# Moving the low half of every sixth expert weight quarter from VectorE to GpSimd

## The reference, cut to what matters

```python
def hier_moe(h, w_rg, b_rg, w_re, b_re, w1, w3, w2):
    """Top-1 group, then top-2 experts inside the chosen group; weight = p_group * p_expert."""
    ...
    comb = jnp.sum(jax.nn.one_hot(eid, N_EXPERTS, dtype=jnp.float32) * wts[..., None], axis=1)
    act = jax.nn.silu(jnp.einsum("nd,edf->nef", xt, w1)) * jnp.einsum("nd,edf->nef", xt, w3)
    act = act * comb[:, :, None].astype(act.dtype)
    y = jnp.einsum("nef,efd->nd", act, w2)
    return y.reshape(bsz, s, d)
```

## Time and profile before

| What | Value |
|---|---|
| median of three runs | 809.09 us (809.0 to 810.13) |
| the profiled execution, its own time | 808.32 us |
| its span | 806.3 us |
| mean granted TensorE clock | 0.993 of full speed |
| TensorE matmul busy | 787.6 us (98%) |
| VectorE busy | 468.5 us (58%) |
| ScalarE busy | 435.6 us (54%) |
| GpSimd busy | 449.2 us (56%), of which 9.59 us after 600 us |
| expert stage | from about 614 us to 799 us of the span |

### The profile page before, as it was taken

One profiled execution on the slowest core, in us unless ns is written; L12 is line 12 of the kernel. 1 busy time (PEld: TensorE's weight loads), 2 busy tenths in 40 slices (PEclk: granted clock), 3 DMA queues, 4 the chain that ended last, 5 costly groups with the idle time before them and its releaser, 6 DMA issues.

```text
span 806.3 us, 15714 instructions
## 1 busy us (share of the span) xinstructions
PE 787.6 (98%) x6063; PEld 705.5 (88%) x6063; DVE 468.5 (58%) x947; ACT 435.6 (54%) x680; POOL 449.2 (56%) x351
## 2 busy tenths in 40 slices
PE   9999999999999999999999999999998999999996
PEld 8999889999999998889999999999986878788784
DVE  5753454672412215486498944437638796795874
ACT  5434654745545456785449533234426675674753
POOL 4997486999999997877974524245832000000002
PEclk9999999999999999999999999999998999999998
DMA  8765145455654554445663312132406896696721
GB/s 296 270 209 209 59 151 183 160 207 208 208 208 163 202 206 165 159 150 179 201 202 119 106 54 90 70 106 106 144 1 270 356 355 270 239 400 230 297 87 52
DMA packets 22522, 148.14 MB, mean 184 GB/s; under 512 B 2624, under 2 KB 3136, under 8 KB 5568
## 3 DMA queue, kind: packets, MB, share of 16 engines
q1 hardware_dynamic: 21024, 144.11, 49.1%
q10 hardware_dynamic: 1440, 3.21, 1.3%
HBM read 144.82 MB, written 1.05 MB: 181 GB/s over the span
## 4 chain that ended last, share of the span: by engine, by line
PE 92%; DVE 4%; DMA 1%; ACT 1%; issue 1%; SPq 0%; DVEq 0%; ACTq 0%
PE bank L1268 77%; PE bank L1839 3%; DMA raw<-weights_dram 1%; DVE w_lo L3038 1%; PE bank L1421 1%; PE bank L1435 1%; PE bank L1371 1%; PE bank L1868 0%; PE bank L2083 0%; PE bank L1927 0%; PE bank L2123 0%; PE bank L1444 0%; PE bank L1445 0%; PE bank L1533 0%; PE bank L1809 0%
## 5 line engine op out<-in xcount | busy, mean ns | idle before, releaser
L659 POOL TENSOR_TENSOR w_lo<-raw,w_hi 128x512 fp32r<-128x512 f32 x340 | 439.5, 1328 | 151.8 <-ACT w_hi L711 141.7
L1268 PE MATMUL bank<-h_hi,w_hi 128*128 128x256 f32 x800 | 227.8, 285 | 0.1
L1268 PE MATMUL bank<-h_hi,w_lo 128*128 128x256 f32 x800 | 222.8, 279 | 0.0
L1268 PE MATMUL bank<-h_lo,w_hi 128*128 128x256 f32 x788 | 219.0, 278 | 0.0
L711 ACT ACTIVATE w_hi<-raw 128x1024 fp32r<-128x1024 f32 x170 | 173.6, 1059 | 65.2 <-PE bank L1268 34.9
L1268 PEld LDWEIGHTS bank<-h_hi,w_hi 128*128 128x128 f32 x800 | 150.6, 188 | 4.5 <-issue 1.7
L1268 PEld LDWEIGHTS bank<-h_hi,w_lo 128*128 128x128 f32 x800 | 150.5, 188 | 0.0
L1268 PEld LDWEIGHTS bank<-h_lo,w_hi 128*128 128x128 f32 x788 | 148.4, 188 | 0.3
L1268 PE MATMUL bank<-w_hi,g 128*128 128x512 f32 x360 | 115.8, 392 | 3.2 <-issue 1.6
L690 POOL TENSOR_TENSOR tok<-x_sb,work 128x512 f32<-128x512 f32 x2 | 2.5, 1288 | 185.6 <-DVE x_sb L3142 185.6
L1268 PEld LDWEIGHTS bank<-w_hi,g 128*128 128x128 f32 x360 | 67.6, 188 | 17.7 <-issue 2.0
(11 more groups left out here) (421 smaller groups left out, 1314.8 us busy)
## 6 DMA issues: line engine op xcount, KB each, us to landing
raw<-weights_dram SPq DMA_DIRECT2D x108, 1024.0 KB, 4.8
work<-weights_dram SPq DMA_DIRECT2D x24, 1024.0 KB, 6.9
raw<-weights_dram SPq DMA_DIRECT2D x4, 512.0 KB, 5.9
x_sb<-x_dram SPq DMA_DIRECT2D x2, 512.0 KB, 4.4
work<-final_norm_dram ACTq DMA_DIRECT2D x2, 512.0 KB, 3.9
work<-work ACTq DMA_DIRECT2D x8, 128.0 KB, 6.5
out_dram<-tok SPq DMA_DIRECT2D x3, 256.0 KB, 2.3
work<-constants_dram SPq DMA_DIRECT2D x1, 640.0 KB, 6.9
```

Of the source, the lines that this page charges most:

```text
L659: return nc.gpsimd.tensor_tensor(w_lo[:, part], raw[:, part], w_hi[:, part].bitcast(F32), ALU.subtract)
L1268: ins = mm(dst, a, b, start=start and n == 0, stop=stop and n == 2, skip_group_check=True)
```

## The change

The low half of every quarter with q = 5, 16 of the 96, is made by GpSimd in one instruction of 1024 columns. VectorE makes the other 80. GpSimd takes them in stream order behind `tok_lo`, each when the high half of that quarter is done. The semaphore `tok_lo_done` is renamed `pool_lo_done` and counts on from 2. TensorE waits for the semaphore of the engine that makes the quarter; SP waits for both before it loads over a raw half. What each quarter computes, the rings, the order on ScalarE and the steps of TensorE stay as they are.

```diff
+POOL_QUARTERS = (5,)
+
+def by_pool(j):
+    return STREAM[j][1] in POOL_QUARTERS
+
+def lows(j, pool):
+    return sum(by_pool(i) == pool for i in range(j + 1))
...
                 if h >= SLOT_RING:
-                    sp.wait_ge(sem("slot_lo_done"), 2 * (h - SLOT_RING) + 2)
+                    last = 2 * (h - SLOT_RING) + 1
+                    sp.wait_ge(sem("slot_lo_done"), lows(last, False))
+                    if lows(last, True):
+                        sp.wait_ge(sem("pool_lo_done"), NT + lows(last, True))
...
-                ins.then_inc(sem("tok_lo_done"), 1)
+                ins.then_inc(sem("pool_lo_done"), 1)
+            for j in range(len(STREAM)):
+                if by_pool(j):
+                    (hi_, lo_), of = slot_ring(j), slot_quarter(j)
+                    pool.wait_ge(sem("slot_hi_done"), j + 1)
+                    nc.gpsimd.tensor_tensor(lo_, of, hi_.bitcast(F32), ALU.subtract).then_inc(sem("pool_lo_done"), 1)
...
+            def await_low(j):
+                if by_pool(j):
+                    pe.wait_ge(sem("pool_lo_done"), NT + lows(j, True))
+                else:
+                    pe.wait_ge(sem("slot_lo_done"), lows(j, False))
...
                     else:
-                        pe.wait_ge(sem("slot_lo_done"), j + 1)
+                        await_low(j)
...
-                pe.wait_ge(sem("slot_lo_done"), j + 1)
+                await_low(j)
...
-            pe.wait_ge(sem("slot_lo_done"), len(STREAM))
+            for k in range(2):
+                await_low(streamed(LAST_UNIT, 4 + k))
...
-                    if p == SPLIT_AT[j]:
+                    if p == SPLIT_AT[j] and not by_pool(j):
                         slot_low(j)
```

More of the change, by code:

```diff
@@ L687, in _ @@
                 pool.wait_ge(sem("expert_constants"), 32)
-                pool.wait_ge(sem("tok_lo_done"), NT)
+                pool.wait_ge(sem("pool_lo_done"), NT)
                 pool.wait_ge(sem("x_summed"), c + 5)
@@ L2130, in _ @@
                 if p == 2:
-                    pe.wait_ge(sem("tok_lo_done"), NT)
+                    pe.wait_ge(sem("pool_lo_done"), NT)
                     gather(tok_lo, False, True)
```

## The result

The changed kernel takes 815.16 us (median of four runs, 813.74 to 817.13), the kernel before 809.05 in the same comparison: a ratio of 1.0079, with a 95% interval from 1.0065 to 1.0093. It is slower by 6.1 us. 815.6 us had been forecast, by the case of turns at SBUF and at least one fall of TensorE's clock. One execution further down, of the changed kernel with later splits, took 3419.99 us; nothing on record explains it, and its ratio leaves it out.

A forecast was written before the change was run, and what follows sets the result against it. TensorE, busy 98% of the span, was taken as the bound. Longer stalls (3.2 us), lost time between bunches (0.1) and clock falls (3.2) summed to 6.5 us on 809.09: 815.6 us, range 811.2 to 819.0.

The forecast's parts named there:

- the case of turns at SBUF and at least one fall of TensorE's clock: Likeliest case: GpSimd and VectorE alternate at SBUF, stalls grow, clock falls after two of three; 815.6 us, chance 0.50.
- The bound and the three places: TensorE busy 98%; stalls before down steps of units 2, 8 and 14, behind large bunches of low halves, are what matters.
- The turns: VectorE's two-input SBUF low halves and GpSimd's exclude each other; one GpSimd turn costs VectorE 2.2 us.
- The delay of a bunch: VectorE's low halves before units 2, 8 and 14: 2.2 added, 1.14 removed, +1.07 us each, 3.2 us for three.
- The length of GpSimd's instruction: GpSimd's low half of 1024 columns: between 2.27 and 2.57 us, taken as 2.4 us.
- The rival in which VectorE keeps the port: GpSimd waits until the low halves before units 2, 8 and 14 are done; 1.7 us faster, 807.4 us, chance 0.07.
- The clock: TensorE's clock falls to 1.2 GHz behind two of three stalls, 1.6 us each: 3.2 us, ends 0 and 4.8.
- Between the bunches: VectorE catching up in the units after each large stall: 0.1 us lost in all.
- The walk: VectorE's time between activation low halves against TensorE's allowance: 8.93 against 8.94 us for unit 3, 8.54 against 8.43 for unit 4.
- The sum: Whole kernel: 3.2 + 0.1 + 3.2 = 6.5 us over the median of 809.09, giving 815.6 us.
- the case's own range: Likeliest case: 813.8 us with one clock fall to 817.8 us with three and a longer GpSimd instruction.
- What could be gained: Stalls before units 2, 8 and 14: about 4.6 us removable in all; without added turns, 0.57 us gained at each.

The follow-up runs named there:

- later splits: Changed kernel with every split at the earliest four steps ahead of its first use, not up to six: 806.17 us, ratio 0.9962.
- the kernel with three handovers: Changed kernel with GpSimd making only quarters 15, 45 and 75, VectorE the other 93: 815.43 us, ratio 1.0064.
- the one with thirteen: Changed kernel with GpSimd making the q = 5 quarters except 15, 45 and 75, which stay on VectorE: 810.16 us, ratio 1.0006.
- where TensorE was kept busy: Changed kernel plus 16 zero-weight matmuls before TensorE's wait for the activation's low half of units 2, 8 and 14: 812.84 us, ratio 1.0055.
- the two pieces: Changed kernel with each GpSimd low half made in two instructions of 512 columns: 814.99 us, ratio 1.0076.
- the low half left out: Changed kernel with no engine making q = 5 low halves; GpSimd fills one column and signals, TensorE takes the high half twice: 807.76 us, ratio 0.9978.
- the fill: Changed kernel with GpSimd filling 1728 unused SBUF columns instead of making q = 5 low halves; TensorE takes the high half twice: 807.13 us, ratio 0.9968.

## Why the prediction was right

**The bound and the three places.** Right. Only the waits in front of the down steps of units 2, 8 and 14 mattered, as the kernel with three handovers shows from one side and the one with thirteen from the other.

**The turns.** Right, in kind and in size at the places that counted. The delay of a bunch was worked out as 2.2 - 1.14 = 1.07 us. It is 1.07 in the first bunch of the changed kernel, and 1.06, 1.08 and 1.07 where TensorE was kept busy. The length of GpSimd's instruction, bounded by 2.27 and 2.57 and taken at 2.4 us, is 2.40; the estimate of 2.36 drawn from a page lay near it too. The stalls of 2.5 to 2.7 us are 2.44, 2.73 and 2.67. The rival in which VectorE keeps the port is out for the bunches: in all three GpSimd went in when the low half before it ended (quarters 14, 44 and 74), and VectorE stood without a high half at that moment. It does happen elsewhere, in the 4.58 us at 673.46, where it helped and cost nothing.

**The clock.** Right that it falls, and the price of 1.6 us is that of the profile (2.69 - 1.08 and 2.66 - 1.07). That it would be after two of three stalls was a guess. In the three kernels with bare stalls of this length (the changed one, the three handovers, the two pieces) it fell at 5 of 9, once for 6.6 us and more, and twice the fall began before TensorE had resumed. At the twelve stalls of 0.79 to 1.64 us in the kernels before, with thirteen quarters, with the low half left out and with the fill it did not fall. The Trainium skill (TensorE: Matmul & The Clock Gate, section "HAM oscillation — how this bites in real kernels") warns only of longer idle gaps than these, and by it the clock would have held; here the runs speak against it.

**Between the bunches.** Under-sized. The step gave 0.1 us in all; the profile has 0.29 + 0.12, and 0.86 where the clock was held. The walk itself came true for unit 3: from one activation low half to the next it is 661.88 - 652.94 = 8.94 us, 8.93 forecast. But a wait that is missed by a hair has a price of its own, which the walk put at nothing:

```profile
661.94 0.39 PE L1289 MATMUL bank<-w_hi,slot_lo 128*128 128x512 f32 x1
662.35 0.50 PE L1289 MATMUL bank<-w_hi,g 128*128 128x512 f32 x1
```

The gap between these two is 0.02 us, yet the second starts 0.41 us after the first, where the stream has 0.228, and the 24 matmuls from there take 5.74 us against 24 x 0.228 = 5.47. With thirteen handovers the term was 1.45 us, not the up to 0.6 that was expected of that run, 1.03 of it at unit 5, where quarters 33 and 35 put two turns in front of one activation low half; the walk counted one for each. In the changed kernel the second of them fell behind it. With later splits the term was 2.6 us in place of nothing: a turn that falls on low halves not yet needed also pushes back the activation's low half that stands behind them in VectorE's queue.

**The sum.** That 815.16 comes so near to 815.6 is in part luck. Five falls in nine, at 1.6 us, make 2.7 us for three stalls where 3.2 was taken, an estimate; the term between the bunches was too small by 0.3 to 0.8 us. The two errors nearly cancel. The low end of the case's own range, for one fall, adds up to 809.09 + 3.3 + 1.6 = 814.0 and not 813.8.

**What could be gained.** The 0.57 us per bunch without turns is what the kernel with the low half left out gained. But "about 4.6 us" as the whole of the stalls was too low: without them TensorE is 5.5 us ahead, since each stall costs 0.25 to 0.32 us beyond its idle time, as in 5.76 us for 24 matmuls where 36 take 8.21.

## What to carry to other kernels

Before moving a two-input elementwise operation from VectorE to GpSimd, look what VectorE runs beside it: if that reads two tiles of SBUF as well, the move can take from VectorE nearly the length of GpSimd's instruction, here 2.2 us for the 1.14 us saved, because the two work in turn and not side by side. A stall behind a bunch of work is first a question of order: putting off the work with slack by two steps removed all three stalls, with no engine added. And a stall that grows can cost twice, by the clock behind it.

## What the runs showed of the hardware that had not been expected

- A fill of 1728 columns (1.55 us) on GpSimd beside VectorE's two-input reads costs neither anything.
- Idle gaps of TensorE of 2.4 to 2.7 us were followed by or ran into the 1.2 GHz level at 5 of 9 places in otherwise busy matmul streams, gaps of 0.79 to 1.64 us at 0 of 12; with 16 matmuls with a zero weight tile in the gap the clock stayed at 1.00 at 3 of 3.
- VectorE can keep GpSimd waiting through two or three of its two-input instructions: 4.58 us, and twice 5.79 us, for a subtraction that takes 2.40 alone, each time when the two began within 0.05 us of each other.
- A stall of TensorE costs 0.25 to 0.32 us more than the idle time that the profile gives it. Part of it is how rows count: a matmul's row lasts 0.39 us while in the stream the next starts after 0.228. The rest is the first matmul behind the gap, whose successor starts after 0.31 to 0.34 us (709.48 to 709.79, 764.57 to 764.91).
